# Three products of high and low parts in place of float32 products in an output and a query projection

## The chip, the cores and the metric

The kernel runs on 1 core of one Trainium2 chip. The metric is the device time of one execution in microseconds (us); lower is better.

## The reference

One inference step of a decoder layer, for 512 prompt tokens and 8 x 4 sample tokens (T = 544 in all), model width D = 1024, in float32. What matters here is its last third:

```python
mix = concatenate([o_attn, y_pool], axis=-1)              # (T, 1024)
h = x + einsum('tc,cd->td', mix, w_out)                   # output projection
xt = rmsnorm(h, norm2_g)
q = einsum('td,dc->tc', xt, peer_wq)                      # query projection, 2048 columns: 8 heads x 2 halves x 128
s = einsum('thcd,hckd->thck', q, peer_subkeys)            # scores against 128 keys for each of the 16 halves
sv, si = top_k(s, 16); cand = sums of pairs; cv, ci = top_k(cand, 16)   # 16 experts of 16384 per head and token
a = gelu(einsum('td,thkd->thk', xt, expert_u[expert]))
y = h + einsum('thk,thkd->td', softmax(cv) * a, expert_v[expert])
```

The two einsums with `w_out` and `peer_wq` are what the change touches. Everything before them (norm, input projection, attention in three branches, pooling mixer) is as it was.

## The kernel before, in words

Activations are kept transposed: 8 pieces of 128 model rows by 544 token columns. The kernel is a chain of blocks, each with programs written out by hand for the engines, with semaphores between them: `project`, `attend`, `output_and_queries` (line 1094, the one that changes) and `experts` (line 1404). SP issues most DMAs, in its program's order, and stops at each wait.

**The weight ring.** Three buffers of 128 x 1024 float32 (512 KB each) take in turn the tiles of `w_in`, `w_out` (8), `peer_wq` (16), `expert_u` (128) and `expert_v` (128).

**`output_and_queries`.** An output tile m is the products of weight tile m with all 8 pieces of `mixT`, in two halves of 272 token columns (TensorE, `output`, L1152): 16 float32 products. VectorE adds it to the residual `xT` (L1241) and multiplies by the norm's gain (`hg`, L1243); ScalarE squares (L1298); a product with a matrix of 1/D gives the mean of the squares (`mean`, L1159). After the eighth, ScalarE takes the root (L1300) and VectorE the reciprocal (L1245). A query tile i of 16 is the same kind of product, of `peer_wq` with `hg` (`project`, L1173). VectorE multiplies it by the reciprocal root (L1253). TensorE then makes the scores of the tile before (`score`, L1188 to 1191), ScalarE and VectorE copy them out (L1308, L1258, L1259). Between these VectorE makes the normed input `xn` and its low part (L1275, L1279), ScalarE its high part (L1315). The order of one iteration on VectorE is: query, scores, input, then parts of the search for the best experts (`best`, `pairs`, `best_pairs`, from L1360): on every second i two rows of 128 scores of the last 128 tokens (`Sr`), on the others the pairs of one head. For i = 9 to 14 (EARLY = 6 steps) a step of two rows of token tile 0 (`S0`) comes as well. SP loads the next ring tile when `tile_mm` says that the tile three back was used (L1125); `subkeys` (1 MB) go out at the fifth output tile (L1134).

**`experts`.** 128 units multiply the first 384 tokens with `expert_u`, 128 more with `expert_v`, and the other tokens' chosen experts are gathered row by row by POOL (L1532) and dotted or added on VectorE (L1741, L1752). In each unit ScalarE rounds the ring tile to fp32r (`w_hi`, L1542), VectorE takes what is left (`w_lo`, L1632), and TensorE sums hi x hi, hi x lo and lo x hi: 24 products of 384 columns. In the first pass VectorE also does the remaining search steps of the three token tiles: 45 - EARLY of them, placed by `dense_step_unit` in units 9 to 83 or so, and one-hot products (L1838) build the gates. In the second pass each unit's hidden rows are loaded back six units ahead (`load_hidden`, L1487, 112 of them), with NHS = 8 semaphores in turn; VectorE multiplies them by the gates (L1628, semaphore `gated`), then makes `w_lo`. SP's order in one iteration v of the second pass is: a piece of gates (L1481), the ring tile v (L1497), the hidden rows of v + 6 (L1487):

```python
def load_hidden(i):                                        # i = v - NU + AHEAD
    u = v_order[i]
    sp.wait_ge(gated, i - NHS + 1)
...
    if v >= NRAW:
        sp.wait_ge(w_lo, v - NRAW + 1)
        sp.dma_start(ring(v)[:, :], w).then_inc(loaded(v)[0], 16)
...
    if NKEEP <= v - NU + AHEAD < NU:
        load_hidden(v - NU + AHEAD)
```

Of the kernel before, what the change touches and what calls it, by code (L numbers as in the profile page):

```python
# [16 lines left out]
P = 128  # L17
# [92 lines left out]
def bank(g, k, n=1):  # L110
    return g.ps[:, 512 * k:512 * (k + n)]
# [982 lines left out]
def output_and_queries(nc, g):  # L1094


    with ExitStack() as ctx:
        sb, sem = memory(nc, ctx)
        NQ = 2 * PH
        keys = sb("sub_keys", [P, NQ, NKEY])  # L1100
        norm2 = sb("norm2", [P, KC])
        sq = sb("sq2", [P, 2, T])
        rstd = sb("rstd2", [P, T])
        hg = sb("h_gained", [P, KC, T])
        xn = sb("xn2", [P, KC, T])
        qp = sb("q_peer", [P, 2, T])
        n_in, k_in = sem("n2_in"), sem("keys_in")
        tile_mm, h_added, hg_ready, q_out = map(sem, ("tile_mm", "h_added", "hg_ready", "q_out"))
        sq_ready, sq_used, std_ready, rstd_ready, xn_ready, hi_ready = map(sem, (
            "sq2_ready", "sq2_used", "std2_ready", "rstd2_ready", "xn2_ready", "hi_ready"))  # L1110
        s_mm, s_act, s_dve, y_mm, y_out, x_mm, h_stored, chain, x4_ready = map(sem, (
            "ps_mm", "ps_act", "ps_dve", "rows_y_mm", "rows_y_out", "rows_x_mm", "quad_h_stored", "c_chain", "x4_ready"))
# [3 lines left out]
        x4 = sb("quads_T", [P, 2, KC, 4, NQR])  # L1116
        block = ctx.enter_context(nc.Block())

        @block.sync
        def _(sp):  # L1120
            sp.dma_start(norm2[:, :], g.a["norm2"]).then_inc(n_in, 16)
            for t in range(RING_OUT + 2, RING_U + 3):
                if t >= RING_OUT + 3:

                    sp.wait_ge(tile_mm, t - 3 - RING_OUT + 1)  # L1125
                if t < RING_Q:
                    w = g.a["w_out"][t - RING_OUT]
                elif t < RING_U:
                    w = g.a["peer_wq"][t - RING_Q]
                else:  # L1130
                    w = g.a["expert_u"][t - RING_U]
                sp.dma_start(g.ring[t % 3][:, :], w).then_inc(g.ring_in[t % 3], 16)
                if t == RING_OUT + 4:
                    sp.dma_start(keys[:, :, :], g.a["subkeys"]).then_inc(k_in, 16)  # L1134
                if t == RING_Q + 6:
                    sp.wait_ge(y_out, 2)
                    sp.dma_start(g.a["quad_h"], g.quad_x[:, :]).then_inc(h_stored, 16)

        @block.tensor
        def _(pe):  # L1140
            def weights(t):
                pe.wait_ge(g.ring_in[t % 3], 16 * (t // 3) + 16)
                return g.ring[t % 3]

            def output(m):
                w = weights(RING_OUT + m)
                if m >= 2:

                    pe.wait_ge(h_added, m - 1)
                for h in range(2):  # L1150
                    for k in range(KC):
                        last = nc.tensor.matmul(bank(g, 2 * (m % 2) + h)[:, 0:HALF], w[:, k * P:(k + 1) * P],  # L1152
                                                g.mixT[:, k, h * HALF:(h + 1) * HALF], start=(k == 0), stop=(k == KC - 1))
                last.then_inc(tile_mm, 1)
# [8 lines left out]
            def project(i):  # L1163
                w = weights(RING_Q + i)
# [4 lines left out]
                for k in range(KC):  # L1169
                    if i == 0:  # L1170
                        pe.wait_ge(hg_ready, k + 1)
                    for h in range(2):
                        last = nc.tensor.matmul(bank(g, 2 * (i % 2) + h)[:, 0:HALF], w[:, k * P:(k + 1) * P],  # L1173
                                                hg[:, k, h * HALF:(h + 1) * HALF], start=(k == 0), stop=(k == KC - 1))
                last.then_inc(tile_mm, 1)
# [26 lines left out]
            last.then_inc(y_mm, 1)  # L1202
            for i in range(1, NQ):
                project(i)
                if i == 1:
                    pe.wait_ge(y_out, 1)
                    pe.wait_ge(x4_ready, 1)
                    for k in range(KC):
                        last = nc.tensor.matmul(bank(g, 6 + k // 4)[:, (k % 4) * P:(k % 4 + 1) * P], x4[:, 0, k].rearrange("p q t -> p (q t)"),
                                                g.c["c_ident"][:, :], start=True, stop=True)  # L1210
                    last.then_inc(y_mm, 1)
                score(i - 1)
# [5 lines left out]
            last.then_inc(x_mm, 1)  # L1218
# [5 lines left out]
            last.then_inc(x_mm, 1)  # L1224
# [11 lines left out]
        def _(dve):  # L1236
            dve.wait_ge(n_in, 16)
# [7 lines left out]
            nc.vector.reciprocal(rstd[:, :], rstd[:, :]).then_inc(rstd_ready, 1)  # L1245
            dve.wait_ge(rstd_ready, 1)
# [14 lines left out]
            n_chain = [0]  # L1261

            def link(ins):

                n_chain[0] += 1
                ins.then_inc(chain, 1)
                dve.wait_ge(chain, n_chain[0])
# [25 lines left out]
        def _(act):  # L1293
            for k in range(KC):
                act.wait_ge(h_added, k + 1)
# [5 lines left out]
            act.wait_ge(y_mm, 1)  # L1301
            nc.scalar.activation(g.rows_y[:, :], bank(g, 6, 2), ACT.Copy).then_inc(y_out, 1)
            act.wait_ge(y_mm, 2)
# [12 lines left out]
            act.wait_ge(x_mm, 1)  # L1316
            nc.scalar.activation(g.rows_x[:, :], bank(g, 0, 2), ACT.Copy)
            act.wait_ge(x_mm, 2)
# [8 lines left out]
EARLY = 6  # L1327


def dense_step_unit(d):  # L1330

    return 9 + (d - EARLY) * 76 // 39

# [70 lines left out]
def experts(nc, g):  # L1404


    with ExitStack() as ctx:
# [4 lines left out]
        NRAW, NROW, NGB, NHS = 3, 4, 2, 8  # L1412
# [569 lines left out]
```

## Time and profile before

| | |
|---|---|
| median of 3 runs | 1877.61 us (1876.81 to 1883.81) |
| the profiled execution | 1873.63 us, its span 1871.8 us |
| TensorE busy | 1757.5 us (94%) |
| VectorE busy | 1357.4 us (73%) |
| ScalarE, GpSimd busy | 705.9 us, 430.6 us |
| DMA | 457.28 MB moved, mean 244 GB/s |
| stages (from the timeline) | project and attend to 427 us, output tiles to 492, query tiles to 635, end of the block to 644, experts' first pass to 1317, second to 1871.8 |

How to read it: times of the trace count from the start of the span. PE is TensorE's products, PEld its weight loads, DVE VectorE, ACT ScalarE, POOL GpSimd, SP the engine that issues most DMAs. A float32 product is two instructions in the trace, one on fp32r data a single one. Products are pipelined, so the time of one is read from the distance of starts and not from its length. "[x <-y]" is idle time x of the engine before the instruction, ended by y.

### The profile page before, as it was taken

The numbers are of one execution on the slowest core, as the hardware profiler recorded it, in microseconds if no ns is written. First come the engines' busy times: TensorE is split into PE (matmuls) and PEld (weight loads), VectorE is DVE, ScalarE is ACT, GpSimd is POOL, SyncE is SP. The second block draws the span as 40 slices with busy tenths as digits, with TensorE's granted clock in tenths as the row PEclk, the third lists the DMA queues.
The fourth block names the chain that finished last, engine by engine and source line by source line (L and its number), as shares of the span: only waits on it lengthen the run. The fifth ranks groups of instructions, "written<-read, shape, count | busy, mean of one in ns | idle before, by whom it ended". The sixth has DMA issues, their size and how long they took to land.

```text
span 1871.8 us, 29166 instructions
## 1 busy us (share of the span) xinstructions
PE 1757.5 (94%) x10248; PEld 1635.8 (87%) x10248; DVE 1357.4 (73%) x2739; ACT 705.9 (38%) x1348; POOL 430.6 (23%) x341
## 2 busy tenths in 40 slices
PE   8994888889999979999899999999899999999999
PEld 6873676668888879999799999999899899999999
DVE  2163334661146799999999998786699899989986
ACT  1111244430110233355666576663333333333333
POOL 0000000000000013322322233334244443445440
PEclk9897899899999989999899999999999999999999
DMA  9213321222221258887789789999799999999995
GB/s 289 72 50 132 105 68 52 80 75 81 67 68 57 84 182 303 292 297 272 259 292 329 267 297 337 360 355 358 255 381 396 341 402 394 392 375 390 390 395 181
DMA packets 199252, 457.28 MB, mean 244 GB/s; under 512 B 25842, under 2 KB 106226, under 8 KB 198642
## 3 DMA queue, kind: packets, MB, share of 16 engines
q1 hardware_dynamic: 127474, 256.34, 39.8%
q0 software_dynamic: 46192, 172.13, 24.5%
q10 hardware_dynamic: 25440, 26.93, 4.1%
q8 instruction: 82, 1.34, 0.3%
q14 instruction: 64, 0.52, 0.1%
HBM read 402.71 MB, written 56.05 MB: 245 GB/s over the span
## 4 chain that ended last, share of the span: by engine, by line
PE 43%; DVE 15%; DMA 3%; issue 3%; ACT 2%; SPq 0%; DVEq 0%; ACTq 0%; POOLq 0%
PE ps L1816 8%; PE ps L1819 8%; PE ps L1822 8%; PE ps L1792 6%; PE ps L1788 5%; PE ps L1789 5%; DVE sb_w_lo L1632 3%; PE ps L1838 3%; DMA sb_ring<-expert_v 3%; DVE sb_one_hot L1734 1%; DVE sb_hot L1659 1%; DVE sb_slot L1660 1%; DVE sb_hot L1655 1%; DVE sb_expert_row L1741 1%; DVE sb_scores L1741 1%
## 5 line engine op out<-in xcount | busy, mean ns | idle before, releaser
L1542 ACT ACTIVATE sb_w_hi<-sb_ring 128x1024 fp32r<-128x1024 f32 x256 | 271.3, 1060 | 506.1 <-PE ps L1792 222.0
L1632 DVE TENSOR_TENSOR sb_w_lo<-sb_ring,sb_w_hi 128x1024 fp32r<-128x1024 f32 x256 | 313.0, 1223 | 85.2 <-ACT sb_w_hi L1542 83.8
L1788 PE MATMUL ps<-sb_x_hi,sb_w_hi 128*128 128x384 f32 x1024 | 352.5, 344 | 2.1 <-ACT sb_w_hi L1542 2.1
L1789 PE MATMUL ps<-sb_x_lo,sb_w_hi 128*128 128x384 f32 x1024 | 347.8, 340 | 0.0
L1792 PE MATMUL ps<-sb_x_hi,sb_w_lo 128*128 128x384 f32 x1024 | 209.1, 347 | 29.0 <-DVE sb_w_lo L1632 29.0
L1792 PEld LDWEIGHTS ps<-sb_x_hi,sb_w_lo 128*128 128x128 f32 x1024 | 186.4, 193 | 33.3 <-DVE sb_w_lo L1632 33.1
L1816 PE MATMUL ps<-sb_x_lo,sb_w_hi 128*128 128x384 f32 x1016 | 199.6, 338 | 11.1 <-ACT sb_x_lo L1549 11.1
L1819 PE MATMUL ps<-sb_x_lo,sb_w_lo 128*128 128x384 f32 x1016 | 198.4, 337 | 0.0
L1822 PE MATMUL ps<-sb_x_lo,sb_w_hi 128*128 128x384 f32 x1016 | 197.3, 336 | 0.0
L1788 PEld LDWEIGHTS ps<-sb_x_hi,sb_w_hi 128*128 128x128 f32 x1024 | 194.4, 190 | 2.4 <-ACT sb_w_hi L1542 2.4
L1789 PEld LDWEIGHTS ps<-sb_x_lo,sb_w_hi 128*128 128x128 f32 x1024 | 194.5, 190 | 0.0
L1816 PEld LDWEIGHTS ps<-sb_x_lo,sb_w_hi 128*128 128x128 f32 x1016 | 178.5, 189 | 15.0 <-issue 11.1
L1819 PEld LDWEIGHTS ps<-sb_x_lo,sb_w_lo 128*128 128x128 f32 x1016 | 179.6, 189 | 0.0
L1822 PEld LDWEIGHTS ps<-sb_x_lo,sb_w_hi 128*128 128x128 f32 x1016 | 178.7, 188 | 0.0
L1532 POOL DMA_INDIRECT sb_scores<-expert_u_rows,sb_row_expert x80 | 98.1, 1226 | 320.2 <-DVE sb_row_dots L1741 217.3
L1532 POOL DMA_INDIRECT sb_expert_row<-expert_u_rows,sb_row_expert x80 | 104.1, 1301 | 209.9 <-DVE sb_row_dots L1741 203.5
L1532 POOL DMA_INDIRECT sb_scores<-expert_v,sb_row_expert x80 | 111.1, 1389 | 167.9 <-DVE sb_rows_y L1752 98.7
L1569 ACT ACTIVATE sb_one_hot<-sb_one_hot,sb_slotT 128x128 f32<-128x128 f32 x384 | 117.6, 392 | 58.8 <-DVE sb_one_hot L1734 56.3
L1532 POOL DMA_INDIRECT sb_expert_row<-expert_v,sb_row_expert x80 | 109.6, 1369 | 131.1 <-DVE sb_rows_y L1752 98.3
L1173 PE MATMUL ps<-sb_h_gained,sb_ring 128*128 128x272 f32 x512 | 121.4, 395 | 0.0
L1173 PEld LDWEIGHTS ps<-sb_h_gained,sb_ring 128*128 128x128 f32 x512 | 96.0, 190 | 21.7 <-issue 2.8
L267 PE MATMUL ps<-sb_scores,sb_ring 128*128 128x272 f32 x416 | 99.2, 399 | 0.0
(310 smaller groups left out, 2481.6 us busy)
## 6 DMA issues: line engine op xcount, KB each, us to landing
sb_ring<-expert_u SPq DMA_DIRECT2D x128, 512.0 KB, 5.7
sb_ring<-expert_v SPq DMA_DIRECT2D x128, 512.0 KB, 8.1
gates_dense<-sb_g_stage ACTq DMA_DIRECT2D x12, 2048.0 KB, 16.0
hid_dense<-sb_hid SPq DMA_DIRECT2D x112, 192.0 KB, 5.2
sb_scores<-hid_dense SPq DMA_DIRECT2D x112, 192.0 KB, 7.5
sb_g_stage<-gates_dense SPq DMA_DIRECT2D x32, 384.0 KB, 7.1
sb_g_stage<-gates_dense SPq DMA_DIRECT2D x48, 256.0 KB, 9.1
sb_region<-cache_cmp SPq DMA_DIRECT2D x64, 128.0 KB, 2.0
```

Of the source, the lines that this page charges most:

```text
L267: last = nc.tensor.matmul(bank(g, b + h)[:, 0:HALF], g.ring[t % 3][:, k * P:(k + 1) * P], xg[:, k, h * HALF:(h + 1) * HALF], start=(k == 0 ...
L1173: last = nc.tensor.matmul(bank(g, 2 * (i % 2) + h)[:, 0:HALF], w[:, k * P:(k + 1) * P], hg[:, k, h * HALF:(h + 1) * HALF], start=(k == 0), ...
L1532: pool.indirect_dma_start(out=row[j % NROW][:, :], out_offset=None, in_=table, in_offset=bass.IndirectOffsetOnAxis(ap=row_e[:, n:n + 1], a ...
L1542: nc.scalar.activation(whi[v % 2][:, :], ring(v)[:, :], ACT.Copy).then_inc(w_hi, 1)
L1569: last = nc.scalar.activation(oh[n % 2][:, 1, t], oh[n % 2][:, 1, t], ACT.Copy, scale=slotT[:, 2, TB * n + t:TB * n + t + 1])
L1632: nc.vector.tensor_tensor(wlo[v % 2][:, :], ring(v)[:, :], whi[v % 2][:, :], ALU.subtract).then_inc(w_lo, 1)
L1788: nc.tensor.matmul(out, hi[:, c * P:(c + 1) * P], g.x_hi[:, c], start=(c == 0), stop=False)
L1789: nc.tensor.matmul(out, hi[:, c * P:(c + 1) * P], g.x_lo[:, c], start=False, stop=False)
L1792: last = nc.tensor.matmul(out, lo[:, c * P:(c + 1) * P], g.x_hi[:, c], start=False, stop=(c == KC - 1))
L1816: nc.tensor.matmul(out(m), hi[:, m * P:(m + 1) * P], chi[u % 2], start=(u == 0), stop=False)
L1819: nc.tensor.matmul(out(m), lo[:, m * P:(m + 1) * P], chi[u % 2], start=False, stop=False)
L1822: last = nc.tensor.matmul(out(m), hi[:, m * P:(m + 1) * P], clo[u % 2], start=False, stop=False)
```

## The change

It makes the two projections in the way of the experts. Weights and inputs are split into a high part (rounded to fp32r by ScalarE) and a low part (the rest, by VectorE), and a tile is the sum of three runs of 16 products: hi x hi, hi x lo, lo x hi. The high and low weights have two buffers each. The inputs are split once: `mixT` at the start of the stage, `hg` as it is made. `xn` is now made from `xT`, gain and reciprocal root in one operation. Ring buffers come free at the low part. The keys share memory with the split `mixT` and load after the last output tile. EARLY goes from 6 to 4, the four steps now at i = 9, 11, 13, 15, and the other 41 are spread over nearly the same units. To free semaphores, three are merged into one (`rows_mm`) and NHS goes from 8 to 7.

```diff
+        with ExitStack() as first:
+            mix = [memory(nc, first)[0](f"mix_{n}", [P, KC, T], F32R) for n in ("hi", "lo")]
...
+        hg = [sb(f"h_gained_{n}", [P, KC, T], F32R) for n in ("hi", "lo")]
+        whi = [sb(f"wc_hi{k}", [P, KC * P], F32R) for k in range(2)]
+        wlo = [sb(f"wc_lo{k}", [P, KC * P], F32R) for k in range(2)]
...
         @block.sync
...
-                    sp.wait_ge(tile_mm, t - 3 - RING_OUT + 1)
+                    sp.wait_ge(lo_made, t - 3 - RING_OUT + 1)
...
-                if t == RING_OUT + 4:
+                if t == RING_Q + 2:
+                    sp.wait_ge(tile_mm, KC)
                     sp.dma_start(keys[:, :, :], g.a["subkeys"]).then_inc(k_in, 16)
...
         @block.tensor
+            def product(c, x, first):
+                hi, lo = whi[c % 2], wlo[c % 2]
+                at = lambda h: bank(g, 2 * (c % 2) + h)[:, 0:HALF]
+                half = lambda h: slice(h * HALF, (h + 1) * HALF)
+                pe.wait_ge(hi_made, c + 1)
+                for k in range(KC):
+                    if first:
+                        pe.wait_ge(hi_split, first + k)
+                    for h in range(2):
+                        nc.tensor.matmul(at(h), hi[:, k * P:(k + 1) * P], x[0][:, k, half(h)], start=(k == 0), stop=False)
+                for k in range(KC):
+                    if first:
+                        pe.wait_ge(lo_split, first + k)
+                    for h in range(2):
+                        nc.tensor.matmul(at(h), hi[:, k * P:(k + 1) * P], x[1][:, k, half(h)], start=False, stop=False)
+                pe.wait_ge(lo_made, c + 1)
+                for k in range(KC):
+                    for h in range(2):
+                        last = nc.tensor.matmul(at(h), lo[:, k * P:(k + 1) * P], x[0][:, k, half(h)], start=False, stop=(k == KC - 1))
+                last.then_inc(tile_mm, 1)
...
         @block.vector
+            def low_part(c):
+                dve.wait_ge(hi_made, c + 1)
+                if c >= 2:
+                    dve.wait_ge(tile_mm, c - 1)
+                nc.vector.tensor_tensor(wlo[c % 2][:, :], g.ring[(RING_OUT + c) % 3][:, :], whi[c % 2][:, :], ALU.subtract).then_inc(lo_made, 1)
+
+            for k in range(KC):
+                dve.wait_ge(hi_split, k + 1)
+                nc.vector.tensor_tensor(mix[1][:, k], g.mixT[:, k], mix[0][:, k], ALU.subtract).then_inc(lo_split, 1)
+                if k == 5:
+                    low_part(0)
             dve.wait_ge(n_in, 16)
             for m in range(KC):
+                low_part(m + 1)
                 dve.wait_ge(tile_mm, m + 1)
...
-                nc.vector.tensor_scalar(hg[:, m], g.xT[:, m], norm2[:, m:m + 1], None, ALU.mult).then_inc(hg_ready, 1)
+                dve.wait_ge(hi_split, KC + m + 1)
+                nc.vector.scalar_tensor_tensor(out=hg[1][:, m], in0=g.xT[:, m], scalar=norm2[:, m:m + 1], in1=hg[0][:, m],
+                                               op0=ALU.mult, op1=ALU.subtract).then_inc(lo_split, 1)
...
             for i in range(NQ):
+                if KC + i + 1 < NC:
+                    low_part(KC + i + 1)
                 project(i)
...
-                    nc.vector.tensor_tensor(xn[:, i - 1], hg[:, i - 1], rstd[:, :], ALU.mult).then_inc(xn_ready, 1)
+                    nc.vector.scalar_tensor_tensor(out=xn[:, i - 1], in0=g.xT[:, i - 1], scalar=norm2[:, i - 1:i], in1=rstd[:, :],
+                                                   op0=ALU.mult, op1=ALU.mult).then_inc(xn_ready, 1)
...
-                if KC < i <= KC + EARLY:
-                    h = i - KC - 1
+                if KC < i and i % 2:
+                    h = (i - KC) // 2
                     dve.wait_ge(s_act, 2 * h + 2)
                     best(S0, (2 * h, 2 * h + 1), g.sv0, g.si0)
...
         @block.scalar
+            def high_part(c):
+                t = RING_OUT + c
+                act.wait_ge(g.ring_in[t % 3], 16 * (t // 3) + 16)
+                if c >= 2:
+                    act.wait_ge(tile_mm, c - 1)
+                nc.scalar.activation(whi[c % 2][:, :], g.ring[t % 3][:, :], ACT.Copy).then_inc(hi_made, 1)
+
+            high_part(0)
+            for k in range(KC):
+                nc.scalar.activation(mix[0][:, k], g.mixT[:, k], ACT.Copy).then_inc(hi_split, 1)
...
             for k in range(KC):
+                high_part(k + 1)
                 act.wait_ge(h_added, k + 1)
+                nc.scalar.activation(hg[0][:, k], g.xT[:, k], ACT.Copy, scale=norm2[:, k:k + 1]).then_inc(hi_split, 1)
...
 +            high_part(KC + 1)
...
             for i in range(1, NQ):
+                if KC + i + 1 < NC:
+                    high_part(KC + i + 1)
                 score(i - 1)
...
-EARLY = 6
+EARLY = 4
...
-    return 9 + (d - EARLY) * 76 // 39
+    return 9 + (d - EARLY) * 76 // 41
...
-        NRAW, NROW, NGB, NHS = 3, 4, 2, 8
+        NRAW, NROW, NGB, NHS = 3, 4, 2, 7
```

## Rows read from the trace of the kernel before

**Rows 1.** Busy us (count) by stage: PE, PEld, DVE, ACT, POOL; granted clock, DMA share, GB/s.
```profile
427.00:492.00 65.00, 64.95 (x284) 53.89 (x285) 9.07 (x15) 4.60 (x7) 0.00 (x0) 1.00 0.27 81
492.00:635.00 143.00, 141.68 (x688) 116.92 (x687) 78.13 (x330) 15.75 (x27) 3.33 (x8) 1.00 0.22 63
644.00:1105.00 461.00, 432.01 (x2534) 427.59 (x2535) 448.77 (x1039) 242.77 (x499) 123.09 (x97) 0.96 0.78 271
1317.00:1871.00 554.00, 540.54 (x3077) 536.35 (x3075) 480.93 (x577) 195.70 (x258) 217.80 (x158) 0.99 0.95 358
```

**Rows 2.** Timeline of TensorE, output and query tiles (start us, length us).
```profile
450.96 7.50 PE L1152 MATMUL ps<-sb_scores,sb_ring 128*128 128x272 f32 x32
...
459.21 7.50 PE L1152 MATMUL ps<-sb_scores,sb_ring 128*128 128x272 f32 x32
...
540.51 7.60 PE L1173 MATMUL ps<-sb_h_gained,sb_ring 128*128 128x272 f32 x32
...
549.27 7.60 PE L1173 MATMUL ps<-sb_h_gained,sb_ring 128*128 128x272 f32 x32
```

**Rows 3.** Waits, 644 to 1105 us (waited for: us, times, longest us).
```profile
PE ps L1792 <- DVE sb_w_lo L1632: 29.0, 13, 5.0
```

**Rows 4.** Timeline of TensorE, second pass over the experts.
```profile
1541.64 1.56 PE L1819 MATMUL ps<-sb_x_lo,sb_w_lo 128*128 128x384 f32 x8
1543.04 1.56 PE L1822 MATMUL ps<-sb_x_lo,sb_w_hi 128*128 128x384 f32 x8
```

**Rows 5.** Timeline of TensorE, first pass, around a wait.
```profile
697.92 2.93 PE L1792 MATMUL ps<-sb_x_hi,sb_w_lo 128*128 128x384 f32 x8 [3.13 <-DVE sb_w_lo L1632]
...
700.64 0.52 PE L1788 MATMUL ps<-sb_x_hi,sb_w_hi 128*128 128x384 f32 x1
700.96 0.52 PE L1789 MATMUL ps<-sb_x_lo,sb_w_hi 128*128 128x384 f32 x1
```

**Rows 6.** Busy time and granted clock of the same place.
```profile
700.00:702.00 2.00, 2.00 (x8) 2.00 (x8) 1.93 (x13) 1.06 (x2) 1.02 (x1) 0.50 0.90 332
```

**Rows 7.** Chain that ended last, in order of time, first pass.
```profile
1146.85 1.78 PE ps L1838 x16
```

**Rows 8.** Timeline of all engines, second pass.
```profile
1566.75 1.23 DVE L1632 TENSOR_TENSOR sb_w_lo<-sb_ring,sb_w_hi 128x1024 fp32r<-128x1024 f32 x1 [0.37 <-ACT sb_w_hi L1542]
...
1568.01 0.33 SPq L1497 DMA_DIRECT2D sb_ring<-expert_v  x1
...
1571.02 0.55 DVE L1628 TENSOR_TENSOR sb_hot<-sb_scores,sb_g_stage 128x384 f32<-128x384 f32 x1
...
1571.61 0.32 SPq L1487 DMA_DIRECT2D sb_scores<-hid_dense  x1
...
1578.23 1.06 ACT L1542 ACTIVATE sb_w_hi<-sb_ring 128x1024 fp32r<-128x1024 f32 x1 [2.72 <-PE ps L1822]
```

**Rows 9.** Timeline of VectorE and ScalarE, an output tile.
```profile
442.00 0.72 DVE L1241 TENSOR_TENSOR sb_xT_sb<-sb_xT_sb,ps 128x544 f32<-128x544 f32 x1 [6.00 <-PE ps L1152]
...
442.75 0.66 ACT L1298 ACTIVATE sb_sq<-sb_xT_sb 128x544 f32<-128x544 f32 x1 [6.61 <-DVE sb_xT_sb L1241]
```

**Rows 10.** Timeline of VectorE, a query tile.
```profile
585.51 0.22 DVE L1380 TENSOR_TENSOR sb_cand<-sb_sv 128x64 f32<-128x64 f32 x1
...
587.50 0.49 DVE L1363 MAX8 sb_sv<-sb_scores 128x8 f32<-128x128 f32 x2
...
590.05 0.28 DVE L1373 FIND_INDEX8 sb_si<-sb_sv,sb_left 128x8 uint32<-128x128 f32 x1
```

**Rows 11.** Timeline of VectorE, end of the stage.
```profile
642.02 0.29 DVE L1258 COPY sb_scores<-ps 128x128 f32<-128x128 f32 x1 [2.47 <-PE ps L1191]
642.32 0.30 DVE L1259 COPY sb_scores<-ps 32x128 f32<-32x128 f32 x1
```

**Rows 12.** Landing of ring loads, 1332 to 1352, then 1510 to 1640 us.
```profile
DMA to landing us min/median/max: 3.5/3.6/4.4
...
DMA to landing us min/median/max: 5.8/8.3/12.9
```

More of the change, by code:

```diff
@@ L1099, in output_and_queries @@
         NQ = 2 * PH
+        with ExitStack() as first:
+            mix = [memory(nc, first)[0](f"mix_{n}", [P, KC, T], F32R) for n in ("hi", "lo")]
         keys = sb("sub_keys", [P, NQ, NKEY])
+        xn = sb("xn2", [P, KC, T])
+        x4 = sb("quads_T", [P, 2, KC, 4, NQR])
+        qp = sb("q_peer", [P, 2, T])
         norm2 = sb("norm2", [P, KC])
@@ L1103, in output_and_queries @@
         rstd = sb("rstd2", [P, T])
-        hg = sb("h_gained", [P, KC, T])
-        xn = sb("xn2", [P, KC, T])
-        qp = sb("q_peer", [P, 2, T])
+        hg = [sb(f"h_gained_{n}", [P, KC, T], F32R) for n in ("hi", "lo")]
+        whi = [sb(f"wc_hi{k}", [P, KC * P], F32R) for k in range(2)]
+        wlo = [sb(f"wc_lo{k}", [P, KC * P], F32R) for k in range(2)]
         n_in, k_in = sem("n2_in"), sem("keys_in")
[L1108 to L1112, printed above, removed]
+        tile_mm, h_added, q_out = map(sem, ("tile_mm", "h_added", "q_out"))
+        hi_made, lo_made, hi_split, lo_split = map(sem, ("wc_hi_made", "wc_lo_made", "hi_split", "lo_split"))
+        NC = KC + NQ
+        sq_ready, sq_used, std_ready, xn_ready, hi_ready = map(sem, (
+            "sq2_ready", "sq2_used", "std2_ready", "xn2_ready", "hi_ready"))
+        s_mm, s_act, s_dve, rows_mm, y_out, h_stored, chain, x4_ready = map(sem, (
+            "ps_mm", "ps_act", "ps_dve", "rows_mm", "rows_y_out", "quad_h_stored", "c_chain", "x4_ready"))
         Sr = g.Sr.rearrange("p (i n) -> p i n", n=NKEY)
@@ L1140, in _ @@
         def _(pe):
-            def weights(t):
-                pe.wait_ge(g.ring_in[t % 3], 16 * (t // 3) + 16)
-                return g.ring[t % 3]
+            def product(c, x, first):
[18 more added lines that the diff above has]
+                last.then_inc(tile_mm, 1)
             def output(m):
-                w = weights(RING_OUT + m)
                 if m >= 2:
                     pe.wait_ge(h_added, m - 1)
[L1150 to L1154, printed above, removed]
+                product(m, mix, 0 if m else 1)
             def mean(k):
@@ L1163, in project @@
             def project(i):
-                w = weights(RING_Q + i)
                 if i >= 2:
@@ L1168, in project @@
                     pe.wait_ge(h_added, KC - 1 + i)
[L1169 to L1175, printed above, removed]
+                product(KC + i, hg, 0 if i else KC + 1)
             def score(i):
@@ L1201, in _ @@
                                         g.c["c_ident"][:, :], start=True, stop=True)
-            last.then_inc(y_mm, 1)
+            last.then_inc(rows_mm, 1)
             for i in range(1, NQ):
@@ L1210, in _ @@
                                                 g.c["c_ident"][:, :], start=True, stop=True)
-                    last.then_inc(y_mm, 1)
+                    last.then_inc(rows_mm, 1)
                 score(i - 1)
@@ L1217, in _ @@
                                         g.c["c_ident"][:, :], start=True, stop=True)
-            last.then_inc(x_mm, 1)
+            last.then_inc(rows_mm, 1)
             pe.wait_ge(q_out, NQ)
@@ L1223, in _ @@
                                         g.c["c_ident"][:, :], start=True, stop=True)
-            last.then_inc(x_mm, 1)
+            last.then_inc(rows_mm, 1)
             score(NQ - 1)
@@ L1236, in _, with link @@
         def _(dve):
+            n_chain = [0]
+            def link(ins):
+                n_chain[0] += 1
+                ins.then_inc(chain, 1)
+                dve.wait_ge(chain, n_chain[0])
+            def low_part(c):
[8 more added lines that the diff above has]
+                    low_part(0)
             dve.wait_ge(n_in, 16)
             for m in range(KC):
+                low_part(m + 1)
                 dve.wait_ge(tile_mm, m + 1)
@@ L1300, in _ @@
             nc.scalar.activation(halves(rstd[:, :]), halves(bank(g, 4, 2))[:, :, 0:HALF], ACT.Sqrt, bias=g.c["c_eps"][:, :]).then_inc(std_ready, 1)
-            act.wait_ge(y_mm, 1)
+            high_part(KC + 1)
+            act.wait_ge(rows_mm, 1)
             nc.scalar.activation(g.rows_y[:, :], bank(g, 6, 2), ACT.Copy).then_inc(y_out, 1)
-            act.wait_ge(y_mm, 2)
+            act.wait_ge(rows_mm, 2)
             nc.scalar.activation(g.quad_x[:, :], bank(g, 6, 2), ACT.Copy, scale=0.25).then_inc(y_out, 1)
@@ L1315, in _ @@
                     nc.scalar.activation(g.x_hi[:, i - 1], xn[:, i - 1, 0:ND], ACT.Copy).then_inc(hi_ready, 1)
-            act.wait_ge(x_mm, 1)
+            act.wait_ge(rows_mm, 3)
             nc.scalar.activation(g.rows_x[:, :], bank(g, 0, 2), ACT.Copy)
-            act.wait_ge(x_mm, 2)
+            act.wait_ge(rows_mm, 4)
             act.wait_ge(h_stored, 16)
```

10 lines of the change are left out of this document (2 added, 8 removed).

## The prediction, made before the change was run

> **What bounds the kernel now.** I first read the busy time by stage [rows 1]. The change sits in 427 to 644 us: the output projection up to 492, the query projection to 635, and a tail. There TensorE is busy for 65.0 of 65 and 141.7 of 143 us, VectorE for 9.1 and 78.1, DMA engines for about a quarter. So TensorE alone sets these 217 us. The timeline shows its rhythm [rows 2]: an output tile comes every 459.21 - 450.96 = 8.25 us. That is 36 equal instructions of 272 columns (32 of the tile, 4 of the mean), 0.229 us each, so the tile's own 16 float32 products take 7.34 us. A float32 product is two instructions, and 0.229 us is 544 column times of 2.4 GHz: each runs two passes. A query tile comes every 8.76 us, 7.34 plus 1.42 of scores.
>
> Behind the stage come the experts. In the first pass over them (644 to 1317) VectorE is the tight one up to 1105: busy 448.8 of 461 us [rows 1], and TensorE waits 29.0 us in 13 places for the low parts it makes [rows 3]. In the second pass (from 1317) TensorE is busy 540.5 of 554 us, and the DMA engines 0.95 of the time.
>
> **The change, part by part.**
>
> Products. A tile becomes 48 single-pass products on fp32r operands in place of 32 two-pass instructions. The nearest row is the experts' fp32r product of 384 columns: eight come every 1543.04 - 1541.64 = 1.40 us, 0.175 us each [rows 4]. 384 columns at 2.4 GHz are 0.160, so there are 0.015 us beside them. Where the granted clock is 0.50 (1.2 GHz) [rows 6] the same product takes 700.96 - 700.64 = 0.32 us [rows 5], exactly 384 columns at 1.2 GHz: one pass, and the excess belongs to the high clock only. For 272 columns (0.113 us) I get 0.128 if the excess is fixed, 0.124 if it goes with the columns. I take 0.126: 48 x 0.126 = 6.05 us a tile, 1.29 less than 7.34. The bounds: 0.116, with float32's excess of 0.0025 us (8.25/36 - 0.2267), and 0.175, if a product can't come faster than it does in the experts. That weights are loaded before each of 48 products instead of 32 binds nothing by the nearest row: sixteen float32 instructions with their loads take 1.78 us, 0.111 each [rows 7], under 0.126.
> The Trainium skill, "TensorE: Matmul & The Clock Gate", section "Back-to-back issue gap", gives columns over 2.4 plus 2.5 ns at the full clock. By it a product would take 0.116 us and the sum would be 11 us lower; at 384 columns it says 0.1625 where rows 4 have 0.175, so here the trace disagrees with it, and it is my first rival below.
>
> 23 tiles (all but the first) save 23 x 1.29 = 29.7 us.
>
> First tile. Before, it starts at once. After, ScalarE rounds the weights (1.06 us [rows 8]), then eight pieces of the mixed rows; the nearest operation on 544 columns takes 0.66 [rows 9], so the last is ready after 1.06 + 8 x 0.66 = 6.3 us. VectorE makes the low pieces at 0.72 [rows 9], with the weight part of 1.22 us [rows 8] put in after the sixth: 1.06 + 0.66 + 8 x 0.72 + 1.22 = 8.7 us, then one pair of products (0.25) and the third run of sixteen (2.0): 11.0 us against 7.35, **+3.7**. In this stretch TensorE works perhaps 40% of the time. After a wait of 3.13 us in the experts it went to 1.2 GHz, at the latest from 700 on [rows 5, 6]. If it does so here, some twenty products take 0.227 instead of 0.126: **+2**, between 0 and +5.
>
> VectorE and ScalarE in the stage. Each tile adds 1.22 us of low part and 1.06 of high part. Output tiles: VectorE had 0.72 and a scaling of no more, and will have about 2.7 in 6.97 us; ScalarE's 0.66 becomes about 2.4. Query tiles: the new period is 6.05 + 1.42 = 7.47 us. The fullest iterations of VectorE are the odd ones from 9: low part 1.22, query 0.72, scores 0.6 [rows 11], one head's pairs 587.50 - 585.51 = 2.0 and a step of two top-16 searches, 590.33 - 587.50 = 2.83 us [rows 10], together 7.4; the even ones hold 5.4. The high part is made a tile ahead, and the third run, which needs the low part, starts 4 us into a tile. So both are hidden by TensorE; without that cover the odd iterations cost up to 1 us each. One high part does show: that of tile 9 stands behind the square root and comes 0.2 us after the transposes that now cover that time. At the end one search step and its 2.83 us stand before the last score copies (now at 642.02, after 2.47 us of waiting [rows 11]), which lengthens the tail by 0.4. Together **+0.7**. Slots of the ring come free at the low part rather than at the tile's end, so weight loads start earlier; the 1 MB of keys moves behind the output tiles, 9 us ahead of the first score. I cost both at nothing: DMA is three quarters idle here. The merged semaphores change no order; the normed input's operation, now with gain and root in one, has 544 columns as before, so I leave its 0.72 [rows 9].
>
> Search steps moved. Two of the six steps on tile 0 (EARLY 6 to 4) go from the stage, where they were hidden, into units 9 to 83, where VectorE is the tight engine [rows 1, 3]: 2 x 2.83 = 5.7 us. Some of it fits into gaps: **+5**, between +1 and +8.
>
> One semaphore fewer for the hidden rows (NHS 8 to 7). It looks like nothing, but SP issues in order. The load of hidden rows in iteration v now waits for the gating of unit v - 1, not v - 2, and the expert_v load of iteration v + 1 is queued behind it. Today that load goes out at the end of a low part: low part at 1566.75 + 1.23, load at 1568.01. The next gating ends at 1571.02 + 0.55 = 1571.57, and a hidden load follows it at 1571.61 [rows 8]. So the weight load would go out 3.6 us later. It is wanted at 1578.23, 10.2 us after its issue today, 6.6 then; TensorE stops only at the unit's start, a unit (24 x 0.175 = 4.2) less the rounding and its wait (1.6) later. Landing takes 3.6 us without the row gathers and 8.3 at the median, 12.9 at most, with them [rows 12]. Against a loss: the 8 us are mostly queue, since the same 512 KB need only 3.6 alone, and a load issued 3 us later into a queue 8 us deep lands at about the same time. For one: a wait of ScalarE there blocks VectorE's low part, then its row sums, the next gating and the next load. I take **+3**, with +0 and +30 as ends (half of 100 loads late by 0.6 us).
>
> Sum: -29.7 + 3.7 + 2 + 0.7 + 5 + 3 = **-15.3 us**. The profiled execution took 1873.63 us (span 1871.8 and 1.8 around it): 1858.3. It stands 4.0 below the median of 1877.61, so against the median I predict **1862**.
>
> **The rivals.**
> 1. The excess of 0.015 us is a matter of the 384-column stream alone, and 272 columns go at 0.116: 48 x 0.116 = 5.57, 0.48 less for 23 tiles: 1851. For it: float32 shows 0.0025. Against: fp32r is what changes. 0.12.
> 2. A product with its weight load can't come faster than 0.175 us, because fp32r loads cost what float32 loads don't. Then a tile is 8.4 us, 1.06 more than before: +24.4 instead of -29.7, and 0.8 in the first tile. **1917, slower.** It decides once a product takes over 0.153 us (7.34/48). For it: no fp32r product of another width is in the trace. Against: at 1.2 GHz the same product is purely its columns. 0.08.
> 3. The expert_v loads come late, as above, and the second pass stretches by 10 to 30 us beyond the 3 taken. 1872 to 1892, middle 1880. For it: DMA busy at 0.95, landings up to 12.9. Against: the queue argument. 0.15.
> 4. VectorE's odd iterations and the added wait for ScalarE's high part become the bound of the query tiles, 8.0 us instead of 7.47 in all sixteen: +8, 1870. Against: TensorE needs each result only a tile later. 0.10.
> 5. fp32r is no single pass at 272 columns, or something else holds the stage at its old pace (8.25 and 8.76 us): nothing is saved and the costs remain, 1892. 0.05.
> My forecast: 0.50, between 1850 and 1873.
>
> **How the numbers follow.** A measurement of this kernel can tell about 0.5%, 9.4 us, from no change: below 1868.2 is faster, above 1887.0 slower. Faster: 0.45 of the forecast, rival 1, a little of 3 and 4: 0.64. Slower: rival 2, most of 5 and the far end of 3: 0.15. Same: 0.21. The range leaves out rival 2, the far ends of 3 and most of 5, and the low side of rival 1: 1843 to 1887.
>
> **What would show it.** In the profile after: the 272-column fp32r products 0.126 us apart, 16 in 2.0 us; output tiles every 6.97 and query tiles every 7.47 us; the first tile 11 us long, perhaps at the low clock; VectorE waiting for TensorE in every query tile. TensorE's waits for low parts in 644 to 1105 up from 29 to about 34 us. The expert_v loads issued right behind a gating, their landing down to 5 or 6 us, and the second pass 554 to 557 us long. The prediction is wrong if products stand over 0.14 us apart, if VectorE is busy throughout the query tiles, or if ScalarE's waits for expert_v are followed by waits of TensorE adding over 10 us.

## The result and the profile after

The changed kernel takes 1898.28 us (median of 6 runs, 1896.09 to 1903.22). In the same comparison the kernel before takes 1879.47 us (6 runs, 1872.94 to 1886.64). The ratio is 1.0106 with a 95% interval of 1.0080 to 1.0131: **slower by 19 us**, where 1862, in a range from 1843 to 1887, had been forecast. The profiled execution took 1898.58 us, its span 1896.8.

The busy time by stage of the changed kernel, in the columns of [rows 1]:

```profile
434.50:506.00 71.50, 69.67 (x505) 68.00 (x506) 32.28 (x35) 27.37 (x37) 1.92 (x4) 0.95 0.28 89
506.00:617.00 111.00, 109.68 (x860) 105.06 (x859) 83.67 (x295) 25.40 (x37) 1.70 (x4) 1.00 0.24 77
...
1304.00:1896.00 592.00, 554.93 (x3083) 541.45 (x3081) 481.31 (x577) 193.99 (x258) 216.16 (x159) 0.99 0.91 336
```

The last line is the first sign. The second pass fills 592 us in place of the 554 of [rows 1], TensorE is busy for only 14 us more, and the DMA engines' share falls from 0.95 to 0.91: nothing is used harder, so something waits. To put sizes on it I cut both traces at the same events: TensorE's first product of the stage, its first product of each pass, and VectorE's first addition to the output at the end. By this cut the first pass of the kernel before ends at 1323.2.

| us | start of the stage | stage | first pass | second pass |
|---|---|---|---|---|
| before | 427.0 | 217.0 | 679.2 | 541.8 |
| after | 434.5 | 190.8 | 685.6 | 579.2 |
| difference | +7.5 | -26.2 | +6.4 | +37.4 |
| forecast | 0 | -23.3 | +5 | +3 |

For the kernel after, the stage's start is that of ScalarE's first rounding. The four differences make +25.1, against 1898.58 - 1873.63 = +25.0. The +7.5 ahead of the stage is code that the change doesn't touch; in the profiles of this case, experiments among them, the stage begins anywhere from 426.5 to 434.5 us, so I take it as scatter. The medians, which differ by 19, hold less of it.

**The stage does what was forecast.** TensorE's timeline, output tiles 0, 1, 2 and 3, then a query tile and the next one:

```profile
436.28 4.55 PE L1158 MATMUL ps<-sb_mix_hi,sb_wc_hi 128*128 128x272 f32 x16 [2.35 <-ACT sb_mix_hi L1332]
440.63 3.03 PE L1163 MATMUL ps<-sb_mix_lo,sb_wc_hi 128*128 128x272 f32 x16
443.50 2.16 PE L1167 MATMUL ps<-sb_mix_hi,sb_wc_lo 128*128 128x272 f32 x16
445.50 2.16 PE L1158 MATMUL ps<-sb_mix_hi,sb_wc_hi 128*128 128x272 f32 x16
...
452.21 2.37 PE L1158 MATMUL ps<-sb_mix_hi,sb_wc_hi 128*128 128x272 f32 x16
...
459.13 2.37 PE L1158 MATMUL ps<-sb_mix_hi,sb_wc_hi 128*128 128x272 f32 x16
...
543.32 2.28 PE L1158 MATMUL ps<-sb_h_gained_hi,sb_wc_hi 128*128 128x272 f32 x16
...
550.75 2.28 PE L1158 MATMUL ps<-sb_h_gained_hi,sb_wc_hi 128*128 128x272 f32 x16
```

Sixteen products start 445.50 - 443.50 = 2.00 us apart, 0.125 each. An output tile comes every 459.13 - 452.21 = 6.92 us (8.25 in [rows 2]), a query tile every 550.75 - 543.32 = 7.43 us (8.76).

**The second pass does not.** The longest waits from 1304 to 1896 us, in the form of [rows 3]:

```profile
ACT sb_w_hi L1587 <- DMA sb_ring<-expert_v: 285.7, 101, 8.3
...
DVE sb_w_lo L1677 <- ACT sb_w_hi L1587: 78.7, 74, 6.3
...
PE ps L1861 <- ACT sb_x_lo L1594: 34.6, 39, 5.1
PEld ps L1861 <- ACT sb_w_hi L1587: 29.3, 24, 5.2
```

The same view of the kernel before, its second pass:

```profile
ACT sb_w_hi L1542 <- PE ps L1822: 180.7, 83, 7.2
ACT sb_w_hi L1542 <- DMA sb_ring<-expert_v: 99.2, 39, 4.8
```

And TensorE's own longest wait there:

```profile
PE ps L1816 <- ACT sb_x_lo L1549: 11.1, 9, 5.4
```

Before, ScalarE mostly waits for TensorE to free a buffer, in 83 units of 128. After, it waits for the weights in 101 units, and TensorE's wait grows from 11.1 to 34.6 us: the sign of being wrong that the prediction had named (over 10 us of TensorE's waits behind those of ScalarE). The timeline of the changed kernel, at the place of [rows 8], shows why:

```profile
1568.20 1.06 ACT L1587 ACTIVATE sb_w_hi<-sb_ring 128x1024 fp32r<-128x1024 f32 x1 [3.08 <-DMA sb_ring<-expert_v]
...
1569.48 1.22 DVE L1677 TENSOR_TENSOR sb_w_lo<-sb_ring,sb_w_hi 128x1024 fp32r<-128x1024 f32 x1
...
1571.08 1.28 DVE L1797 SCALAR_TENSOR_TENSOR sb_rows_y<-sb_expert_row,sb_row_gate,sb_rows_y 128x1024 f32<-128x1024 f32 x1
...
1572.28 0.55 DVE L1673 TENSOR_TENSOR sb_hot<-sb_scores,sb_g_stage 128x384 f32<-128x384 f32 x1
...
1572.86 0.32 SPq L1532 DMA_DIRECT2D sb_scores<-hid_dense  x1
...
1573.22 0.43 SPq L1526 DMA_DIRECT2D sb_g_stage<-gates_dense  x1
...
1573.70 0.47 SPq L1542 DMA_DIRECT2D sb_ring<-expert_v  x1
...
1582.22 1.06 ACT L1587 ACTIVATE sb_w_hi<-sb_ring 128x1024 fp32r<-128x1024 f32 x1 [2.93 <-DMA sb_ring<-expert_v]
```

Read it as a loop. A weight tile lands and is rounded (1568.20), its low part is made, a row is added, and the next unit's gating ends at 1572.83. Only then may the hidden rows be loaded (1572.86), and behind them on SP come the piece of gates and the weights for three units on (1573.70). Those weights are rounded at 1582.22, one turn of the loop later: 5.50 us of work and 8.52 from the issue to the rounding, 14.0 for three units. In [rows 8] the low part's end (1567.98) released the weight load by itself (1568.01), and the gating was in no loop with it.

### The profile page after: what moved, and what is told of

The parts are those of the page before. It is cut to its first block, busy times and chain, and to the rows that moved or that the text cites. A ratio compares the mean times of both kernels' runs of the same rounds, so it can differ in the third digit from the quotient of the medians.

```text
span 1896.8 us, 30053 instructions
## 1 busy us (share of the span) xinstructions
PE 1754.1 (92%) x10632; PEld 1648.7 (87%) x10632; DVE 1394.4 (74%) x2771; ACT 735.6 (39%) x1388; POOL 432.9 (23%) x341
## 4 chain that ended last, share of the span: by engine, by line
PE 25%; DVE 19%; DMA 14%; issue 5%; ACT 3%; SPq 1%; DVEq 0%; ACTq 0%
DMA sb_ring<-expert_v 12%; PE ps L1837 6%; PE ps L1833 5%; PE ps L1834 5%; DVE sb_w_lo L1677 4%; PE ps L1883 3%; ACT sb_w_hi L1587 2%; DVE sb_rows_y L1797 2%; PE ps L1861 2%; PE ps L1864 2%; PE ps L1867 2%; DVE sb_hot L1673 1%; DVE sb_x_lo L1680 1%; DVE sb_one_hot L1779 1%; DVE sb_hot L1704 1%
## 5 line engine op out<-in xcount | busy, mean ns | idle before, releaser
L1861 PE MATMUL ps<-sb_x_lo,sb_w_hi 128*128 128x384 f32 x1016 | 204.5, 343 | 34.8 <-ACT sb_x_lo L1594 34.6
L1577 POOL DMA_INDIRECT sb_scores<-expert_u_rows,sb_row_expert x80 | 102.1, 1276 | 317.0 <-DVE sb_row_dots L1786 223.1
L1883 PE MATMUL ps<-sb_one_hot 128*128 128x128 f32 x768 | 98.1, 283 | 0.0
L1883 PEld LDWEIGHTS ps<-sb_one_hot 128*128 128x128 f32 x768 | 97.5, 200 | 0.0
```

Source lines behind the costliest of these rows:

```text
L1577: pool.indirect_dma_start(out=row[j % NROW][:, :], out_offset=None, in_=table, in_offset=bass.IndirectOffsetOnAxis(ap=row_e[:, n:n + 1], a ...
L1861: nc.tensor.matmul(out(m), hi[:, m * P:(m + 1) * P], chi[u % 2], start=(u == 0), stop=False)
L1883: last = nc.tensor.matmul(bank(g, 2 + 2 * (n % 2) + t // 4)[:, (t % 4) * P:(t % 4 + 1) * P], oh[n % 2][:, 1, t], oh[n % 2][:, 0, t], start ...
```

## The experiments

All were compared with the kernel before, whose median was 1877.1 to 1879.6 us in these comparisons. Beside each ratio stands its 95% interval. The length of a stage or a pass is that of one profiled execution.

### What the second pass pays for

**1. The change with AHEAD 5 in place of 6.** The hidden rows are loaded five units ahead, so with seven semaphores their load waits for the gating of unit v - 2 again, as before the change.

```diff
-AHEAD = 6
+AHEAD = 5
```

> The changed kernel with hidden rows loaded five units ahead instead of six, so that their wait asks for the gating of unit v - 2 again, as before the change, with seven semaphores. Theory A (the expert_v load stands in SP's queue behind that wait and goes out 3 to 4 us late): the second pass shrinks from 592 to about 555 us, the expert_v loads go out right at the end of a low part, ScalarE's waits for them fall from 286 us to about 100, and the time is about 1862, ratio to the kernel before 0.99. Theory B (the second pass is stretched by something else: the moved search steps, other places in memory, the phase in which the row gathers meet the loads): about 1898, second pass still near 590.

1857.77 us, ratio 0.9892 (0.9860 to 0.9924). The second pass took 538.5 us, one unit every 4.23 us, and ScalarE's waits:

```profile
ACT sb_w_hi L1587 <- PE ps L1867: 221.1, 95, 5.9
...
ACT sb_w_hi L1587 <- DMA sb_ring<-expert_v: 68.3, 26, 5.0
```

The whole second-pass loss is gone, and with it 40 us of the total (1.0106 - 0.9892 = 0.0214 of 1878). What is left of the change saves 19.4 us by the medians (14 to 26 by the interval); the forecast's sum without its NHS term was -18.3. That they agree to 1 us is in part luck: in the profile the stage gives -26.8, the first pass +4.4 and the second -3.3, together -25.7, and a start of the stage 5.7 us later takes the rest back.

**2 and 3. The kernel before with NHS 7 alone, and with NHS 7 and AHEAD 5.**

```diff
-        NRAW, NROW, NGB, NHS = 3, 4, 2, 8
+        NRAW, NROW, NGB, NHS = 3, 4, 2, 7
```

> The kernel before with one edit alone, seven semaphores for the hidden rows instead of eight. Theory A: the second pass grows by 33 to 40 us, time about 1915, ratio 1.018 to 1.021. Theory B: no change, ratio 1.000.

> The kernel before with seven semaphores and five units ahead. Theory A: ratio 1.000, since the wait is the old one and a hidden load has five units (21 us) for its 7.5 us. If seven semaphores cost by themselves, or five units are too few: ratio above 1.005.

The first took 1917.41 us, 1.0190 (1.0160 to 1.0220), its second pass 579.2 us, that of the changed kernel. (The medians differ by 40.3 us, the ratio gives 35.7.) The second took 1879.68, 1.0007 (0.9988 to 1.0027), its second pass 542.3. So the loss belongs to the one number and to nothing in the projections, and it is not the number of semaphores that costs but the unit whose gating the load waits for. The waits of the first:

```profile
ACT sb_w_hi L1542 <- DMA sb_ring<-expert_v: 290.8, 102, 9.5
```

**4. Only the weight load waits.** The kernel before keeps its eight semaphores. A wait ahead of the weight load alone holds it to the gating that the seven would have it wait for; hidden rows and gates go when they did.

```diff
+                    if NKEEP <= v - 1 - NU + AHEAD < NU:
+                        sp.wait_ge(gated, v - 1 - NU)
                     sp.dma_start(ring(v)[:, :], w).then_inc(loaded(v)[0], 16)
```

> The kernel before with eight semaphores, hidden loads where they were, and only a wait of SP ahead of each expert_v load for the gating that seven semaphores would ask for. It separates the late weight load from the late hidden load. Theory A: as e2, ratio 1.018 to 1.021. If the later hidden load were the cause: ratio 1.000.

1898.35 us, 1.0105 (1.0072 to 1.0139), the second pass 563.9 us: half the ratio that I had expected. SP's part of its timeline:

```profile
1569.75 0.33 SPq L1499 DMA_DIRECT2D sb_ring<-expert_v  x1
1570.51 0.32 SPq L1487 DMA_DIRECT2D sb_scores<-hid_dense  x1
1573.01 0.33 SPq L1499 DMA_DIRECT2D sb_ring<-expert_v  x1
```

The weight load goes first here, on average 2.9 us after the low part that frees its buffer; with NHS 7 hidden rows and gates are issued ahead of it, and it goes 3.5 us after. Three units take 3 x 4.44 = 13.3 us here, and 13.7 with NHS 7. So the late weight load alone carries more than half of the loss (22 of 37 us), and something behind or ahead of it the rest; hence the next run.

**5. The gates wait as well.**

```diff
                 if NKEEP <= v - NU + AHEAD < NU:
                     load_hidden(v - NU + AHEAD)
+                    sp.wait_ge(gated, v - NU)
```

> The kernel before with eight semaphores and the wait of e4, but put right behind each hidden load, so that the piece of gates also waits and goes out just ahead of the expert_v load; only the hidden load keeps its old time. e4 (weight load alone late) stretched the second pass by 22 us, e2 (hidden load, gates and weight load all together) by 37. If what lies ahead of the weight load in the queue makes the rest of the loss, this stands between them, second pass +26 to +35 us, ratio 1.013 to 1.018. If the hidden load's own lateness makes the rest: as e4, ratio 1.010.

1909.91 us, 1.0175 (1.0138 to 1.0212), the second pass 573.0 us. Of the 37 us of NHS 7, 22 come with the late weight load alone (563.9 - 541.8), 9 more when the gates are issued late just ahead of it, and 6 more when the hidden rows are too. The issue of the weights, on average 2.9, 3.0 and 3.5 us behind the low part in experiments 4, 5 and 2, goes the same way. But these are single profiled passes, and the second pass of the seven kernels without the late load ran from 538.5 to 545.8 us. Experiment 4 stands apart from experiment 2; experiment 5 isn't told apart from experiment 2, whose intervals overlap, and hardly from 4. The shares of 9 and 6 us are not shown.

**6. One semaphore fewer still, NHS 6.** Now the load waits for its own iteration's gating, and the loop closes over two units in place of three.

> The kernel before with six semaphores: SP waits for one gating more. A loop sets the pace: three units of time are one landing plus 6.1 us of work (after: 3 x 4.57 = 7.6 + 6.1). With six semaphores the load goes out one unit later, so two units must hold a landing and the 6.1 us. With a landing of 5 to 6 us a unit takes 5.5 to 6.1 us instead of 4.25: second pass +140 to +200 us, ratio 1.075 to 1.105. If the pace is set by the DMA engines' throughput and not by the loop, a unit can't get much slower than with seven: ratio under 1.04.

2081.66 us (two runs), 1.1085 (1.1039 to 1.1131), the second pass 741.9 us, a unit every 6.04 us. It is the largest effect of the study, just above the upper end of what I had expected (1.105, which lies within the interval). The landing of its weight loads from 1510 to 1640 us, the line of [rows 12]:

```profile
DMA to landing us min/median/max: 3.7/6.1/8.7
```

and the same of the changed kernel:

```profile
DMA to landing us min/median/max: 5.0/7.5/9.4
```

The loop can be added up from the traces, piece by piece. The work is the time from the start of a tile's rounding to the issue of the load that it leads to; the slack is the time that a landed tile waits for its rounding. Means over units 141 to 250, in us:

| kernel | work | landing | slack | sum | units spanned x time of a unit |
|---|---|---|---|---|---|
| before | 2.9 | 8.7 | 1.2 | 12.8 | 3 x 4.25 = 12.8 |
| after | 6.1 | 7.5 | 0.1 | 13.7 | 3 x 4.57 = 13.7 |
| NHS 6 | 5.9 | 6.1 | 0.0 | 12.0 | 2 x 6.04 = 12.1 |

Before, the loop has slack, since ScalarE waits for TensorE. With seven semaphores and with six there is none: the loop sets the pace. Turning nearly the same piece of work over in fewer units is what differs. The rival of the expectation, that the DMA engines' throughput sets the pace, falls as well: their share is 0.78 from 1510 to 1640 us, against 0.91 in the changed kernel's second pass. The loads land sooner (3.7 at the least, near the first line of [rows 12]), but not soon enough to leave slack.

### What is left to take

**7. The change with AHEAD 5 and EARLY 6**, the six steps of token tile 0 at i = 9 to 14 as before the change.

```diff
-                if KC < i and i % 2:
-                    h = (i - KC) // 2
+                if KC < i <= KC + EARLY:
+                    h = i - KC - 1
...
-EARLY = 4
+EARLY = 6
...
-    return 9 + (d - EARLY) * 76 // 41
+    return 9 + (d - EARLY) * 76 // 39
...
-        AHEAD = 6
+        AHEAD = 5
```

> The changed kernel, hidden rows five units ahead, with all six search steps back in the stage and the old spread of the rest. Moved steps cost what I said: first pass 5 us shorter (about 679 instead of 684), but VectorE now has 8.2 us in each even query tile from 10 to 14 against TensorE's 7.4, so the stage may give 1 to 3 us back; net 2 to 4 us under e1, ratio 0.987. If the first pass was longer for another reason (scatter, phase): no difference from e1.

1852.11 us, 0.9860 (0.9832 to 0.9887). The stage took 190.4 us, against 190.2 in experiment 1: no cost of two more steps shows in the query tiles, which still come every 7.43 us. The first pass took 680.5 us, against 683.6. The intervals of experiments 1 and 7 overlap, so the whole times don't show the gain; the table below does.

**8. AHEAD 5 and the first output tile by float32 products** from the ring, so that TensorE works while mixed rows and weights are split. The second tile now waits for the split pieces, and high and low weights, and the waits for them, begin with it.

```diff
-                product(m, mix, 0 if m else 1)
+                if m == 0:
...
+                    for h in range(2):
+                        for k in range(KC):
+                            last = nc.tensor.matmul(bank(g, h)[:, 0:HALF], g.ring[t % 3][:, k * P:(k + 1) * P],
+                                                    g.mixT[:, k, h * HALF:(h + 1) * HALF], start=(k == 0), stop=(k == KC - 1))
...
+                product(m, mix, 1 if m == 1 else 0)
```

> The changed kernel, hidden rows five units ahead, and the first output tile made by float32 products straight from the ring while the mixed input is being split. The first tile takes 7.35 us instead of 11.0: 3.6 us less than e1, ratio 0.9873, stage 187 instead of 191 us. If the split itself (ScalarE and VectorE) is not done in 7 us, or the clock falls anyway, less.

1849.06 us, 0.9846 (0.9818 to 0.9874); the stage took 187.5 us. Its start:

```profile
429.26 7.57 PE L1182 MATMUL ps<-sb_scores,sb_ring 128*128 128x272 f32 x32 [0.63 <-PEq L537]
436.47 2.37 PE L1161 MATMUL ps<-sb_mix_hi,sb_wc_hi 128*128 128x272 f32 x16
```

The first tile lasts 7.21 us in place of 445.50 - 434.53 = 11.0 in the changed kernel, and the second starts without a wait. The granted clock stays at 1.00 from 426 to 440 us. The stage is 2.7 us shorter than in experiment 1 and not 3.6: there the first tile took 10.35 us, as its low clock lasted 3.4 us in place of the changed kernel's 6.8.

**9 and 10. All three together, and with EARLY 7.** Nine is AHEAD 5, EARLY 6 and the float32 first tile; ten puts one more step into the stage.

> The three edits together: hidden rows five units ahead, six search steps in the stage, first output tile in float32. The gains add: stage 187.5 us (e8), first pass 681 (e7), second pass 542, so about 1847 against the 1878 of the kernel before, ratio 0.983. If the gains of e7 and e8 over e1 were scatter: ratio near 0.989.

> As e9 with a seventh search step in the stage, in the last query tile. VectorE's 2.83 us leave the first pass, where VectorE is the tight engine, and lengthen the end of the stage by 0.4 us as they did in the changed kernel: 2 us under e9, ratio 0.982, hardly to be told apart in time, but the first pass should be 2 to 3 us shorter. If the moved steps cost nothing in the first pass: no difference there and 0.4 us more in the stage.

Nine took 1849.15 us, 0.9837 (0.9805 to 0.9869), ten 1855.56 us, 0.9883 (0.9855 to 0.9911). Nine beats the change by 2.7% and the kernel before by 1.6%. It is not told apart from eight in time. Of its expectation the stage came true (187.2 us), the first pass didn't (686.9 for 681) and the second came out at 545.8 for 542. Ten missed its 0.982, though the intervals of nine and ten just touch: its stage took 189.1 us, 1.9 more than nine's in place of 0.4. In the query tiles the pace is the same; behind the last one TensorE waits 4.37 us for the experts' first rounded weights, against 2.40 in nine. So the seventh step, in the last query tile, costs time in the stage.

What a moved step costs can't be read from whole first passes: the two EARLY 6 kernels seven and nine took 680.5 and 686.9 us. But the search steps end in unit 83, so I cut the pass at the end of VectorE's low part of unit 84:

```profile
1095.16 1.22 DVE L1632 TENSOR_TENSOR sb_w_lo<-sb_ring,sb_w_hi 128x1024 fp32r<-128x1024 f32 x1
```

in the kernel before (pass from 644.03), and in the changed one (pass from 625.28):

```profile
1080.71 1.22 DVE L1677 TENSOR_TENSOR sb_w_lo<-sb_ring,sb_w_hi 128x1024 fp32r<-128x1024 f32 x1
```

| kernel | EARLY | first pass to there, us | the rest of the pass, us |
|---|---|---|---|
| before; 2 to 6 | 6 | 452.3; 452.8, 452.6, 452.6, 452.6, 452.9 | 226.9; 229.5, 228.4, 229.4, 230.6, 226.9 |
| after, 1, 8 | 4 | 456.7, 456.7, 456.9 | 228.9, 226.9, 229.3 |
| 7, 9 | 6 | 452.3, 453.8 | 228.2, 233.1 |
| 10 | 7 | 453.3 | 233.8 |

The six of the old form agree within 0.6 us, the three with EARLY 4 within 0.2, and they lie 4.1 us higher; seven, the changed kernel with the old steps, is back at 452.3. So the two moved steps cost 4.1 us there, and nothing else in the change shows. Behind unit 84, where no search step was moved, the same work takes anything from 226.9 to 233.8 us: that is where the scatter sits. Why nine and ten are the slowest in both parts, for the steps they have, stays open.

## Why the prediction was wrong, step by step

**Products: right.** 0.125 us measured, 0.126 forecast; an output tile 6.92 us (6.97), a query tile 7.43 (7.47). Rivals 1, 2 and 5 fell with the lines at 443.50 and 445.50 of TensorE's timeline. By the formula of the Trainium skill, "TensorE: Matmul & The Clock Gate", section "Back-to-back issue gap", which that section gives for an isolated product, it would be 0.116: for this stream the trace disagrees with it at 272 columns as [rows 4] did at 384. The excess over the columns is 0.0117 us at 272 and 0.015 at 384, between fixed and proportional as the two ways of working had it.

**First tile and clock: 2.1 us too high.** The forecast was +3.7 and +2 for the clock, +5.7; the measurement is 11.0 - 7.35 = +3.6 in all. Both terms were too high, the splits by some 0.9 and the clock by 1.2; that the tile took the 11.0 us named for it without the clock is luck. The clock did go to its low level, 1.2 GHz. TensorE stood idle from 433.93 to 436.28, until the first weights and the first piece were rounded, and the granted clock, 1.00 until 435.7, is 0.50 from there to 442.5:

```profile
436.00:438.00 2.00, 1.72 (x7) 1.67 (x8) 1.83 (x3) 2.00 (x5) 0.00 (x0) 0.50 0.86 248
438.00:440.00 2.00, 2.00 (x9) 1.83 (x8) 2.00 (x5) 2.00 (x5) 0.00 (x0) 0.50 0.02 6
...
442.00:444.00 2.00, 2.00 (x16) 2.00 (x15) 1.61 (x2) 0.00 (x0) 0.00 (x0) 0.86 0.77 246
```

and splitting went faster than the 0.66 and 0.72 us a piece that I took from [rows 9]:

```profile
435.50 4.46 ACT L1332 ACTIVATE sb_mix_hi<-sb_scores 128x544 fp32r<-128x544 f32 x8
...
436.17 3.90 DVE L1266 TENSOR_TENSOR sb_mix_lo<-sb_scores,sb_mix_hi 128x544 fp32r<-128x544 f32 x6 [2.35 <-ACT sb_mix_hi L1332]
...
441.12 1.35 DVE L1266 TENSOR_TENSOR sb_mix_lo<-sb_scores,sb_mix_hi 128x544 fp32r<-128x544 f32 x2
```

ScalarE takes about 0.55 us a piece and VectorE 0.65. The last low piece is ready at 442.47, so that at the full clock the third run of sixteen could begin 0.25 later, at 442.7. It begins at 443.50: by this estimate the low clock costs 0.8 us, not 2. More products were slow than the twenty that I had counted, but most of them lie within the wait for pieces: two of them take 2 x 0.227 = 0.45 us, and a piece comes every 0.55. The shorter tile of experiment 1 (10.35 us with 3.4 us of low clock) agrees.

**VectorE in the query tiles: right, with less room than named.** It waits for TensorE's tile in 10 of the 16 (9.4 us in all between 506 and 617), not in every one, but the tiles keep their 7.43 us, so rival 4 fell. The whole stage came to -26.2 where products, first tile, clock and small terms had made -29.7 + 3.7 + 2 + 0.7 = -23.3. Of the 2.9 us between them, 2.1 are the first tile's and about 1 that of tiles 0.05 and 0.04 us shorter than forecast.

**Search steps moved: right.** Forecast +5, measured +4.1 by the cut at unit 84. The other 2 us of the first pass's +6.4 lie behind it, within the scatter. The sign named for it was weaker than forecast: TensorE's waits for low parts rose from 29.0 us in [rows 3] to this, and not to 34:

```profile
PE ps L1837 <- DVE sb_w_lo L1677: 30.7, 15, 5.0
```

**NHS 8 to 7: this is the step that failed.** It was booked at +3 and cost 36 (experiment 2: 0.019 of 1878) to 40 us (experiment 1), beyond its own upper end of +30. The mechanism had been found and read rightly: the wait for one gating later, the weight load queued behind it, issued 3.6 us later (3.4 on average by the traces: 3.5 behind the low part in place of 0.1). Rival 3 named it, with 0.15, and its upper end of 1892 was passed too. What failed is the sentence that decided its size, that "a load issued 3 us later into a queue 8 us deep lands at about the same time". Issued 3.4 us later, the load landed after 7.7 us instead of 8.4 at the median over units 141 to 250 (7.5 for 8.7 on average): of 3.4 us only 0.7 to 1.2 came back, where I had expected a landing of 5 or 6 us. So waiting before the issue doesn't replace waiting behind it. What the 8 us consist of, no run takes apart.

The second fault is in the form of the estimate. I compared a load's lead with its landing, once, and counted lateness against TensorE's slack. But a late weight tile delays the low part, that delays the next gating, and that the next load: the delay feeds itself, and once the loop's slack is used up, slack elsewhere can't absorb it. The table of experiment 6 has the account: the work in the loop grew by 3.2 us, shorter landing gave back 1.2 and slack 1.1, and the other 0.9 to 1.0 came on top of three units, 0.32 for each, some 35 us over the 112. With the numbers already at hand the loop could have been summed. Three units have to hold landing plus some 6 us of rounding, low part, row, gating and issues; at 4.2 us a unit that leaves 6.6 us for landing, the very lead that the prediction worked out. The 8.3 us of [rows 12] would have given an upper end, (8.3 - 6.6)/3 x 100 = 57, and no loss at 6.6; the +3 taken needed a median landing of 6.7 us, and in [rows 12] only the quickest loads beside the gathers come under that (5.8 at the least). With the 7.7 measured the same estimate gives 37.

The sum, then: -26.2 in the stage, +6.4 in the first pass and +37.4 in the second, +17.6 against the +19 of the medians. The projections' gain was real and is what experiment 1 shows: 1857.77, 0.9892.

## What to carry to other kernels

A count of semaphores or buffers is also a distance in time: changing it by one moves the event that a load waits for, and everything behind it in the same queue. Write such a wait down as a loop (issue, landing, the work that leads to the next release) and ask whether the units that it spans hold it; if the sum is over, each unit pays its part of the lack. When one limit of a distance is taken away (here a semaphore), take the other down with it (here AHEAD), and the order of waits stays as it was.

## What was not expected of the hardware

A weight load of 512 KB that is issued 3.4 us later, into DMA engines that are busy 0.91 to 0.95 of the time, lands only 0.7 us sooner after its issue (7.7 for 8.4 us at the median). In experiment 6, with a unit only every 6.04 us in place of 4.25 and the DMA engines' share at 0.78, it still took 6.0 us, against 3.6 without the row gathers [rows 12].

Code that no edit touched began the stage anywhere between 426.5 and 434.5 us in twelve profiled executions, and the first pass moved by 6 us between kernels with the same steps in it. A cause of a few microseconds can't be read from the whole length of a pass in one pair of profiles here. Cut at an event just behind the cause (unit 84), six kernels agree within 0.6 us, and 4 us stand out.
